# First modulation as 32-column products on TensorE, a halved filter spectrum, and the second gate pair of retention behind the head's outputs

## What is computed

```python
mod_l = split(silu(c) @ ada_w + ada_b, 6)          # c and ada_w[:, 0:2048] give sh1, sc1 of the tokens
mod_c = split(silu(c_ctx) @ ada_w + ada_b, 6)      # the same weights for the context
hl = rmsnorm(xl, norm1_g) * (1.0 + sc1_l) + sh1_l
hc = rmsnorm(xc, norm1_g) * (1.0 + sc1_c) + sh1_c
```

```python
k = concatenate([h_fwd, zeros_like(h_fwd[:1]), h_bwd[:0:-1]])
y = irfft(rfft(u, n=2 * L) * rfft(k), n=2 * L)[:, :L]
```

```python
q, k, v, g = split(h @ w_in)
o = decayed, causal (q @ k.T) @ v                  # per head
o = o * rsqrt(mean(o * o, axis=-1) + eps)          # over the head's 512 features
out = (silu(g) * o) @ w_out
```

## Time and profile before

| | us |
|---|---|
| median of 3 runs | 2483.89 |
| lowest and highest | 2481.96 and 2486.6 |
| the profiled execution | 2481.02 |
| its span, first to last instruction | 2479.2 |
| TensorE busy in it | 2332.4 |
| VectorE busy | 975.2 |
| ScalarE busy | 524.5 |

### The profile page before, as it was taken

How to read it: one execution, slowest core, us unless ns; L and a number is a source line. 1 busy time by engine, 2 the same in 40 slices (tenths; PEclk the granted TensorE clock), 3 DMA queues, 4 the chain that set the end, 5 groups by cost and what they waited for, 6 DMA issues and landing times.

```text
span 2479.2 us, 28832 instructions
## 1 busy us (share of the span) xinstructions
PE 2332.4 (94%) x10122; PEld 1646.5 (66%) x10123; DVE 975.2 (39%) x1785; ACT 524.5 (21%) x1101; POOL 187.4 (8%) x181
## 2 busy tenths in 40 slices
PE   7989999966889889899999999999999999999999
PEld 3555466542334358678888888576576778888888
DVE  8341466560000043644335423435244344335521
ACT  3200155431111133532111100121211202111100
POOL 1000154200001100000000002102020000000000
PEclk9899999978899999989999999999999999999999
DMA  8401124539796951012222212212021112222230
GB/s 324 157 21 56 51 77 185 197 126 348 300 344 237 345 222 62 27 43 76 83 82 85 83 60 102 111 60 76 25 102 59 51 68 102 86 85 85 86 110 26
DMA packets 81183, 299.08 MB, mean 121 GB/s; under 512 B 9021, under 2 KB 9021, under 8 KB 80462
## 3 DMA queue, kind: packets, MB, share of 16 engines
q1 hardware_dynamic: 75390, 272.31, 31.0%
q0 software_dynamic: 5712, 25.67, 2.8%
HBM read 283.78 MB, written 14.16 MB: 120 GB/s over the span
## 4 chain that ended last, share of the span: by engine, by line
PE 85%; DVE 7%; ACT 3%; issue 2%; DMA 2%; SPq 1%; DVEq 0%; POOL 0%; ACTq 0%; POOLq 0%
PE products L1549 40%; PE products L979 7%; PE products L1379 7%; PE products L1159 6%; PE products L1397 3%; PE products L1454 3%; PE products L1704 2%; PE products L1210 2%; PE products L1631 2%; PE products L1288 1%; PE products L1504 1%; PE products L1223 1%; PE products L1178 1%; DVE weights_and_work L2249 1%; PE products L1199 1%
## 5 line engine op out<-in xcount | busy, mean ns | idle before, releaser
L1549 PE MATMUL products<-normed,weights_and_work 128*128 128x264 f32 (+1 forms) x1520 | 347.7, 384 | 0.0
L1549 PEld LDWEIGHTS products<-normed,weights_and_work 128*128 128x128 f32 x1520 | 288.5, 190 | 49.2 <-issue 3.4
L1379 PE MATMUL products<-weights_and_work 128*64 128x512 f32 x768 | 182.3, 635 | 47.5 <-DMA weights_and_work<-in_experts 46.8
L1800 ACT ACTIVATE weights_and_work<-products 128x256 f32<-128x256 f32 (+4 forms) x227 | 99.7, 457 | 470.7 <-PE products L1549 156.1
L1549 PE MATMUL products<-weights_and_work,mixed 128*128 128x256 f32 (+1 forms) x800 | 182.3, 382 | 0.8 <-ACT weights_and_work L1800 0.8
L1379 PEld LDWEIGHTS products<-weights_and_work 128*64 128x64 f32 x768 | 66.0, 147 | 162.1 <-issue 161.0
L1549 PEld LDWEIGHTS products<-weights_and_work,mixed 128*128 128x128 f32 x800 | 151.8, 190 | 24.4 <-ACT weights_and_work L1800 1.6
L1549 PE MATMUL products<-weights_and_work 128*128 128x256 f32 (+1 forms) x672 | 150.6, 384 | 8.2 <-DVE residual L3134 5.2
L1549 PE MATMUL products<-weights_and_work,normed 128*128 128x264 f32 (+1 forms) x704 | 155.6, 383 | 0.0
L1549 PE MATMUL products<-normed,mixed 128*128 128x264 f32 (+1 forms) x672 | 154.1, 382 | 0.0
L1549 PEld LDWEIGHTS products<-weights_and_work 128*128 128x128 f32 x672 | 128.5, 192 | 29.3 <-issue 7.0
(11 more groups left out here) (543 smaller groups left out, 3025.8 us busy)
## 6 DMA issues: line engine op xcount, KB each, us to landing
weights_and_work<-in_weights SPq DMA_DIRECT2D x303, 512.0 KB, 4.3
weights_and_work<-in_experts SPq DMA_DIRECT2D x192, 512.0 KB, 5.2
results<-normed SPq DMA_DIRECT2D x8, 512.0 KB, 7.0
residual<-in_x POOLq DMA_DIRECT2D x1, 2048.0 KB, 15.0
weights_and_work<-in_dft_half POOLq DMA_DIRECT2D x1, 2048.0 KB, 8.8
token_rows<-mixed SPq DMA_DIRECT2D x4, 512.0 KB, 4.6
normed<-results SPq DMA_DIRECT2D x4, 512.0 KB, 6.7
mixed<-results SPq DMA_DIRECT2D x4, 512.0 KB, 7.4
```

The source lines that it names most:

```text
L1379: m = pe.matmul(ps[UNIT * b:UNIT * (b + 1), side, :], job_t[:, k, UNIT * b:UNIT * (b + 1)], expert_w[b][:, s, at:at + 512], start=(k == 0) ...
L1549: m = pe.matmul(bank(p, n), left(k), right(k), start=(fresh and k == 0), stop=(k == kt - 1), skip_group_check=True)
L1800: act.activation(out, src, ACT.Copy, scale=scale).then_inc(bank_free[p.bank], 1)
```

## The change

It does the following.

- **Modulation on TensorE.** `silu_w` holds silu(c) as weights: for each of the 8 feature tiles 32 columns, of which two are the vectors and 30 are zero. `first_rows` multiplies them by the tiles of `ada_w` as the moving operand: each tile gives two products of 512 columns. A product takes one of the four column groups: the shift's halves take groups 0 and 1, the scale's take 2 and 3, in bank 7. They stand in five portions between the other products of `filters()`. ACT copies the bank to `mod_rows`, four transposes (in place of the 32 one-column products) turn it, and DVE forms `mod1` as before.
- **The order of DVE's work on x.** DVE multiplies x by its root before `mod1` is there, and then does gain and shift in one operation per tile. The context's part stands behind the spectrum's.
- **The spectrum.** The filter's times are ordered even first, then odd. A product over the even times and one over the odd times give frequency k by their sum, and frequency 511 - k by their difference. Two tables' tiles are loaded instead of four, and 16 products of 512 columns are made instead of 32. `mirrored` on DVE makes sum and difference.
- **The stream.** The two tables' tiles stand behind all sixteen tiles of `ada_w`; a slot is released by TensorE's `begun`. The transfer of the small tables (bias, rope and so on) from GpSimd's queue stands behind that of `dft_half`.
- **Retention.** The seven products of g1 stand behind o. DVE adds the four squares, and ms is one product between g1's second and third. The scores' weighted copies `ret_s` and the squares lie in other memory, and `two_halves` is no longer made again for each head.

```diff
 STREAM = [
-    ("mod1_a", 6), ("dft_a", 2),
-    ("mod1_b", 10), ("dft_b", 2),
+    ("mod1", 16), ("dft", 2),
...
+            def first_rows(first, last):
+                p = r["mod1_rows"]
+                if first == 0:
+                    fill(p)
+                    pe.wait_ge(silu_ready, 1)
+                for i in range(first, last):
+                    part, k = i // KT, i % KT
+                    w = weights("mod1", i)
+                    for half in range(2):
+                        o = 32 * (2 * part + half)
+                        m = pe.matmul(ps[o:o + 32, p.bank, :], silu_w[:, k, :], w[:, 512 * half:512 * (half + 1)], start=(k == 0),
+                                      stop=(k == KT - 1), skip_group_check=True)
+                        if half == 0:
+                            begin(m)
...
+            def spectra(kt, c, w):
+                for odd in range(2):
+                    p = r["f_spec"][4 * kt + 2 * (1 - c) + odd]
+                    fill(p)
+                    pe.wait_ge(spec_in, 2 - c)
+                    for tt in range(2):
+                        t = 2 * odd + tt
+                        m = pe.matmul(bank(p), w[:, c, t, :], filt[:, t, :, 0, :] if c == 0 else diff[:, t], start=(tt == 0), stop=(tt == 1))
...
             def modulation():
+                w = dft_tile(0)
+                spectra(0, 1, w)
                 p = r["mod1"]
                 fill(p)
-                pe.wait_ge(mod_read, 16)
-                for i in range(16):
-                    for v in range(2):
-                        m = pe.matmul(ps[:, p.bank, 2 * i + v:2 * i + v + 1], acc1[:, i // 8, v, (i % 8) * P:(i % 8 + 1) * P],
-                                      ones[:, 0:1], start=True, stop=True)
+                read(pe, r["mod1_rows"])
+                for j in range(4):
+                    m = pe.transpose(ps[:, p.bank, j * P:(j + 1) * P], mod_rows[:, j * P:(j + 1) * P], ident)
                 finish(p, m)
-                spectra(3, ST)
+                spectra(0, 0, w)
+                w = dft_tile(1)
+                spectra(1, 1, w)
+                spectra(1, 0, w)
...
# DVE, first stage
-                mod_terms(6, 16)
+                dve.wait_ge(rstd_ready, ROOTS["ms_c"])
+                for k in range(KT):
+                    tt_(h1[:, k, C:], x[:, k, META:T2], rstd[:, 0:S], ALU.mult).then_inc(scaled, 1)
...
+                for k in range(KT):
+                    dve.wait_ge(scaled, k + 1)
+                    ts(h1[:, k, C:], h1[:, k, C:], gain1[:, k, 0:1], mod1[:, k, 0:1], ALU.mult, ALU.add).then_inc(h_ready, 1)
+                for kt in range(2):
+                    mirrored(kt, 1)
+                    mirrored(kt, 0)
...
# TensorE, retention
-                    p, = r["ret", "ms"]
-                    fill(p, it)
-                    for i in range(4):
-                        pe.wait_ge(ret_sqr, it * 4 + i + 1)
-                        m = pe.matmul(bank(p), ones, ret_sq[:, i], start=(i == 0), stop=(i == 3))
-                    finish(p, m)
+                    seven_products(3, it)
...
# in seven_products(j, it), behind P2
+                    if j == 3:
+                        p, = r["ret", "ms"]
+                        fill(p, it)
+                        pe.wait_ge(ret_summed, it + 1)
+                        finish(p, pe.matmul(bank(p), ones, ret_sq[:, 0], start=True, stop=True))
```

325 lines of the change are left out of this document (169 added, 156 removed).

## The result

| | us |
|---|---|
| the kernel before, median of 4 runs | 2485.03 (2481.96 to 2486.6) |
| the changed kernel, median of 4 runs | 2453.22 (2450.1 to 2459.24) |
| ratio, with its 95% interval | 0.9876 (0.9855 to 0.9898) |
| profiled execution, before and after | 2481.02 and 2454.03 |
| its span, before and after | 2479.2 and 2452.2 |

The forecast was 2454.4, range 2448 to 2467. The medians differ by 31.8 us, the two profiled executions by 27.0 only.

A forecast was written before the change was run, and what follows sets the result against it. It took TensorE's chain as the bound, except in the first 85 us, where it ran over DVE's modulation terms; 17.3 (first stage) plus 12.2 (retention) made 29.5 us, from 2483.9 to 2454.4, range 2448 to 2467.

The forecast's parts named there:

- First stage, start: First stage: without two DVE modulation terms the eight filter products start at 16.07 instead of 17.72 and end at 30.0 us.
- Tiles: Modulation: two column groups overlap fully, so a tile takes 0.86 us at the higher clock, sixteen tiles 13.7.
- Clock: First stage: the clock stays low for 4.4 us behind the modulation's first product; the last modulation product ends at 53.1.
- Both rivals on the clock: First stage: clock rises later (10.2 us or more; 2457 to 2461; chance 0.18), or is already up (2452.2; chance 0.03).
- Spectrum: First stage: 16 products take 13.7 us, transposes and changes of shape 0.6, together 14.3; projections start at 67.4.
- Covers: Time ready before wanted: first stage, weights 5 us, DVE 1.2 and 0.7; retention, DVE's sum 1.4, ACT's copy 0.5.
- Retention: Mean square falls from four products to one: 2.6 us a head, 10.4 in four; 12.2 with the last head's end.
- Behind the last head: End of retention: the wait for DVE goes and its half sums start 7.5 instead of 9.3 behind: 1.8 us gained.
- Sum: Whole kernel: 17.3 in the first stage and 12.2 in retention, 29.5 us gained, 2454.4 from the median 2483.9.
- The slower rival: First stage: no overlap and low clock throughout, projections near 115 us, kernel 18 slower, 2502; chance 0.04.

The follow-up runs named there:

- all_rows: The changed kernel with the filter's eight products over all 128 rows of the array instead of 65, the added rows zeros: 2448.56 us, ratio 0.9852.
- spec_twice: The changed kernel with each pair of the spectrum's products made twice, bringing back the 16 removed products: 2470.06 us, ratio 0.9930.
- ms_four: The changed kernel with retention's mean square made by four products again, at its new place, without VectorE's three additions: 2464.66 us, ratio 0.9909.
- sum_in_place: The kernel before with VectorE adding retention's four squares and one mean-square product, at the old place behind the last output: 2485.08 us, ratio 0.9996.
- one_group: The changed kernel with both halves of a modulation tile on the same column group, modulation values wrong: 2443.49 us, first projection at 77.13 us.
- four_groups: The changed kernel with the modulation's shift and scale tiles in turn, so four products can run at once: 2451.77 us, ratio 0.9859.
- all_rows4: The changed kernel with the edits of all_rows and four_groups together: 2444.87 us, ratio 0.9835.
- best: all_rows4 with ScalarE's filter squares ahead of squares of x and more modulation tiles ahead of the filter's sum: 2443.67 us, ratio 0.9835.

## Why the prediction was right, point by point

- **First stage, start.** 30.0 forecast, 29.82 measured.
- **Tiles.** 0.86 a tile where a part is alone: 0.88. Mis-sized: I counted two groups for every tile, but where shift's last tiles meet scale's first, four run at once (0.47 a tile). Four tiles took 1.86 instead of 3.44: 1.6 us of the 2.3 by which the last modulation product came early (50.85, forecast 53.1).
- **Clock.** 4.0 instead of 4.4 us at the lower level. That the clock was still low at 29.82 was read from the rows of before without a reason; all_rows shows that it goes with the filter's 65 rows. That the 4.4 came so near is in part luck, by the spread of 2.4 to 5.0 above. Both rivals on the clock fell.
- **Spectrum.** 14.3 forecast, 65.13 - 50.85 = 14.28 measured; spec_twice confirms what a second half would cost in the changed kernel.
- **Covers.** Weights, VectorE and ScalarE were in time everywhere, with more room than forecast.
- **Retention.** 2.6 a head: 2.57, and ms_four and sum_in_place show both halves of the reason (fewer products, and a place that hides the sum). Behind the last head I missed what the move does to a bank: with its wait of 0.56 the last head gains 1.86 only. The output projection itself brings 1.2 more. Together this is 10.9 in place of 12.2.
- **Sum.** 19.6 + 10.9 = 30.5 in place of 29.5; the errors (2.3 too little in the first stage, 1.3 too much in retention and behind it) had opposite signs. The medians say 31.8 (25 to 36 by the interval). That 2454.4 lies within 1.2 of 2453.22 owes something to the base as well: it was worked out from a median of 2483.89, which with a fourth run became 2485.03.
- **The slower rival**, groups without overlap at the lower clock throughout, had no part that held: one_group has no overlap and is 12 later at the projection, since its clock rises all the same.

## What to carry to other kernels

- When products that leave many of the array's rows empty open a stage, try padding them with rows of zeros: a pass took no longer here, and the clock rose under them (4.7 us of the whole kernel by the medians).
- Put neighbouring 32-column products on different column groups, across the loop's halves too. And when a sum on another engine can replace products, move work between producer and consumer first; without that it was worth nothing over the four heads, instead of 2.6 us a head.
- A gain of a few us early in a kernel can vanish by the clock at later idle stretches (in four_groups' trace 5.0 at 60 us was nothing at 494). Compare starts of the same product along both traces before giving a lost gain a cause, and compare two executions of unchanged code first.

## What the runs showed of the hardware

- Eight products over 65 rows one behind the other: 14.0 us at the lower clock in ten kernels, never a rise. Over 128 rows: 9.6 in all_rows, where the first short record is 5.2 us behind their start, and 8.6 in all_rows4 and best, where it is 3.3. Alternating full-row tiles with 65-row products held the clock low for over 31 us (17.2 to 48.8).
- A modulation tile (two products of 32 columns, two passes each) took 1.72 us on one column group, 0.88 on two, 0.45 with its neighbour on the other two.
- The same waits (0.8 and 1.9 us) in the attention stage were followed by a stretch at the lower clock in four_groups and spec_twice, and by none in the changed kernel. What decides it stays open.
- A wait of 2.17 us ahead of one product of retention, four times in one execution of sum_in_place: the clock fell behind the first and stayed up behind the other three.
